# Hybrid decoder step (two layers, one core): every gathered key and value row is written to the new caches from SBUF, the copies leave these rows out

## The reference, cut to what matters

```python
kk = jnp.concatenate([k_buf, k], axis=1)
vv = jnp.concatenate([v_buf, v], axis=1)
o = dilated_attention(q, kk, vv, k_buf.shape[1])
new_k = kk[:, -n_keep:]
new_v = vv[:, -n_keep:]
```

## Time and profile before

| What | Value |
|---|---|
| Time, median of 3 runs | 415.51 us (415.07 to 419.36) |
| Time of the profiled execution | 418.61 us |
| Its span, first to last instruction | 416.8 us |
| PE matmul busy | 351.3 us (84%) |
| DVE, ACT, POOL busy | 232.5, 99.3, 46.2 us |
| DMA moved | 158.06 MB, mean 379 GB/s |
| HBM read, written | 149.39 MB, 104.42 MB |

### The profile page before, as it was taken

The page is one execution under the profiler, slowest core; times in us unless marked ns, Lnnn a source line. Parts: engine busy times, 40 slices in busy tenths (PEclk is TensorE's granted clock), DMA queues, the critical chain, the costliest instruction groups (busy, mean ns, idle before and its releaser), DMA issues.

```text
span 416.8 us, 4509 instructions
## 1 busy us (share of the span) xinstructions
PE 351.3 (84%) x1536; PEld 270.5 (65%) x1536; DVE 232.5 (56%) x522; ACT 99.3 (24%) x234; POOL 46.2 (11%) x87
## 2 busy tenths in 40 slices
PE   1489799977489979999979999997578969999980
PEld 1378688865367756558868888885356755558860
DVE  0334679749974776430123589849986786331010
ACT  3110014530152422410120021641233422310110
POOL 2300011111101111110100001112010111210000
PEclk9999999996878999999998999998969998999996
DMA  8999999999999999999999999999999999999972
GB/s 288 418 418 418 420 414 370 387 401 390 404 411 418 411 383 411 396 373 362 413 392 416 406 361 402 387 403 393 374 411 415 414 369 403 351 339 338 324 282 84
DMA packets 50676, 158.06 MB, mean 379 GB/s; under 512 B 4724, under 2 KB 20030, under 8 KB 49870
## 3 DMA queue, kind: packets, MB, share of 16 engines
q0 software_dynamic: 21824, 95.11, 59.3%
q1 hardware_dynamic: 19652, 39.36, 25.6%
q10 hardware_dynamic: 9178, 23.31, 14.3%
HBM read 149.39 MB, written 104.42 MB: 609 GB/s over the span
## 4 chain that ended last, share of the span: by engine, by line
SPq 38%; DMA 21%; PE 20%; DVE 16%; issue 2%; ACT 1%; ACTq 0%; DVEq 0%
SPq L380 15%; DMA kv<-in_cache_k_win 13%; DMA out<-kv 8%; PE pj L731 7%; SPq L405 6%; SPq L452 5%; SPq L435 5%; PE pj L592 4%; DVE kv L1096 4%; DVE ssc L1099 4%; PE psc L663 3%; DVE yc L1156 3%; SPq L391 3%; SPq L395 2%; PE ptr L508 2%
## 5 line engine op out<-in xcount | busy, mean ns | idle before, releaser
L592 PE MATMUL pj<-hT,w 128*128 128x264 f32 x800 | 195.6, 403 | 8.6 <-DVE hT L1018 6.0
L592 PEld LDWEIGHTS pj<-hT,w 128*128 128x128 f32 x800 | 157.8, 200 | 40.8 <-issue 10.1
L1156 DVE SCALAR_TENSOR_TENSOR yc<-u_ext,par,yc 128x256 f32<-128x256 f32 x180 | 76.2, 481 | 2.8 <-DVE u_smp L1046 0.6
L731 PE MATMUL pj<-mix,w 128*128 128x264 f32 x256 | 59.5, 387 | 0.0
L731 PEld LDWEIGHTS pj<-mix,w 128*128 128x128 f32 x256 | 48.0, 190 | 8.0
L496 POOL DMA_DIRECT2D out<-in_cache_v_win x48 | 25.8, 543 | 180.2 <-issue 180.2
L1226 DVE TENSOR_TENSOR xT<-xT,pj 128x264 f32<-128x264 f32 x16 | 6.9, 429 | 52.9 <-PE pj L731 52.9
L496 POOL DMA_DIRECT2D out<-in_cache_k_win x32 | 18.6, 584 | 138.4 <-issue 131.3
L840 ACT ACTIVATE ex<-pj 128x264 f32<-128x264 f32 x22 | 8.6, 391 | 82.1 <-PE pj L592 66.3
L663 PE MATMUL psc<-kv,spm 128*48 128x384 f32 x80 | 27.5, 496 | 0.0
L1096 DVE TENSOR_TENSOR kv<-kv,qb 128x1536 f32<-128x1536 f32 x10 | 17.6, 1759 | 10.3 <-DMA kv<-in_cache_k_win 10.0
(11 more groups left out here) (172 smaller groups left out, 322.9 us busy)
## 6 DMA issues: line engine op xcount, KB each, us to landing
out<-in_cache_k_win POOLq DMA_DIRECT2D x32, 1512.0 KB, 75.2
out<-in_cache_v_win POOLq DMA_DIRECT2D x16, 1152.0 KB, 75.4
out<-in_cache_v_win POOLq DMA_DIRECT2D x17, 1080.0 KB, 72.9
w<-in_w_out ACTq DMA_DIRECT2D x2, 4096.0 KB, 28.9
out<-in_cache_v_win POOLq DMA_DIRECT2D x16, 432.0 KB, 73.2
w<-in_w_in SPq DMA_DIRECT2D x2, 3072.0 KB, 32.4
w<-in_w_in ACTq DMA_DIRECT2D x1, 4608.0 KB, 30.7
kv<-in_cache_k_win SPq DMA_DIRECT2D x32, 144.0 KB, 25.1
```

Source lines behind the costliest of these rows:

```text
L592: last = nc.tensor.matmul(pj[n % RING][:, 0:T], wbuf[buf][:, k, col:col + P], hT[:, k, :], start=(k == 0), stop=(k == KD - 1))
L731: last = nc.tensor.matmul(pj[n % RING][:, 0:T], w1[:, k, m * P:(m + 1) * P], mix[:, k, :], start=(k == 0), stop=(k == KD - 1))
L1156: last = V.scalar_tensor_tensor(out=yc[:, t, 0:SEQ], in0=x_w, scalar=par[:, ROW_CW + w * CT + t:ROW_CW + w * CT + t + 1], in1=yc[:, t, 0:S ...
```

## The change

- `put_back` replaces `put_back_values`. Near, mid and far rows of keys and of values are written to the new caches from `kv`. For the far span, output row -1 does not exist, so its first row is left out: 15 partitions of each sample (90 rows) and then 2 DMAs for the 5 remaining rows of the first partition of the samples.
- The copies leave out all gathered rows: 15 of 16 rows up to 1535, 3 of 4 rows of 1536 to 1919, and none of the near ones, for keys and values alike, 48 DMAs a layer.
- On SP the keys' put-backs stand between the load of `w2` and the gather of the values. Each span's put-back waits for its keys (`k_near_in` and so on), and each span's gather of values waits now for the keys' put-back as well as for `ks_used`. The keys' gather of layer 1 waits for the values' put-back span by span.
- The key products no longer overwrite `kv`. They go to `tok4`, one tile that holds `v_tok` and `k_tok`, so DVE waits in layer 1 for these two tiles to have been written out, and ACT's first `vtok` copy waits for the last `sscore`. `sscore` 0, 2 and 3 each wait for one span of keys; before, `sscore` 0 waited for all.
- The last copies of y to SBUF wait for `v_near_out` alone.

```diff
+SPAN_AT = [sum(n for _, _, n in GATHER[:g]) for g in range(len(GATHER))]
+FIRST_CUT = [next(i for i, (a, b) in enumerate(SCORE_CUTS) if b > at) for at in SPAN_AT]
+LAST_CUT = [next(i for i, (a, b) in enumerate(SCORE_CUTS) if b >= at + g[2]) for at, g in zip(SPAN_AT, GATHER)]
...
-COPIES = [("k", s, a, a + HALF_ROWS) for s in range(NS) for a in (0, HALF_ROWS)]
-COPIES += [("v", s, a, b) for s in range(NS) for a, b in ((0, 768), (768, EVEN_ROWS), (FAR_LO, GATHER[0][0]))]
+COPIES = [(kind, s, a, b, d) for kind in "kv" for s in range(NS) for a, b, d in
+          ((0, GATHER[1][0] // 2, GATHER[2][1]), (GATHER[1][0] // 2, GATHER[1][0], GATHER[2][1]),
+           (GATHER[1][0], GATHER[0][0], GATHER[1][1]))]
+SPANS = ("near", "mid", "far")
...
-        v_tok = sb("v_tok", [P, 2, C_ATT])
-        k_tok = sb("k_tok", [P, 2, C_ATT])
+        tok4 = sb("tok4", [P, 4, C_ATT])
+        v_tok, k_tok = tok4[:, 0:2, :], tok4[:, 2:4, :]
...
+            def put_back(kind, l, g):
+
+                name = f"{kind}_{SPANS[g]}_out"
+                out = {"k": o_k_s, "v": o_v_s}[kind][bass.ds(l, 1)]
+                (lo, d, n), at = GATHER[g], SPAN_AT[g]
+                skip = 1 if lo == 0 else 0
+                for s in SAMPLE_ORDER:
+                    r = sample_rows(s)
+                    rows = out[:, s, lo - 1 + d * n * skip:lo - 1 + d * n * PER_S]
+                    rows = rows.rearrange("o (a b e) h d -> (o a) b e (h d)", b=n, e=d)[:, :, 0, :]
+                    sp.dma_start(rows, kv[r.start + 2 * skip:r.stop:2, at:at + n, :]).then_inc(S[name], 16)
+                if skip:
+                    for r in range(2):
+                        rows = out[:, r:NS:2, d - 1:d * n - 1]
+                        rows = rows.rearrange("o s (b e) h d -> (o s) b e (h d)", e=d)[:, :, 0, :]
+                        sp.dma_start(rows, kv[r:P:2 * PER_S, at + 1:at + n, :]).then_inc(S[name], 16)
...
                 sp.wait_ge(x_copied, XROUNDS)
                 if l > 0:
                     sp.wait_ge(S["sc_full"], nth(l - 1, "sc_full", NH + 1))
-                    for name in ("v_near_out", "v_far_out"):
-                        sp.wait_ge(S[name], nth(l - 1, name, per[name]))
-                gather("k", l, "k_in")
+                for g, span in enumerate(SPANS):
+                    if l > 0:
+                        sp.wait_ge(S[f"v_{span}_out"], nth(l - 1, f"v_{span}_out", per[f"v_{span}_out"]))
+                    gather("k", l, g, f"k_{span}_in")
                 if l > 0:
                     sp.wait_ge(S["pj_full"], nth(l - 1, "pj_full", NPROJ))
                 weights(l, w2, 0, "w_in", COL["b_val"], 2 * C_POOL, "b_in")
-                gather("v", l, "v_in", "ks_used")
+                for g, span in enumerate(SPANS):
+                    sp.wait_ge(S[f"k_{span}_in"], nth(l, f"k_{span}_in", per[f"k_{span}_in"]))
+                    put_back("k", l, g)
+                for g, span in enumerate(SPANS):
+                    sp.wait_ge(S["ks_used"], nth(l, "ks_used", LAST_CUT[g] + 1))
+                    sp.wait_ge(S[f"k_{span}_out"], nth(l, f"k_{span}_out", per[f"k_{span}_out"]))
+                    gather("v", l, g, "v_in")
...
                 sp.wait_ge(S["v_in"], nth(l, "v_in", per["v_in"]))
-                put_back_values(l)
+                for g in range(len(SPANS)):
+                    put_back("v", l, g)
...
-                    if a < FAR_LO or kind == "k":
-                        dst = out[l, s, a:b].rearrange("(c e r) h d -> c e (r h d)", c=16, r=PIECE_ROWS)
-                        src = cache[l, s, a + 1:b + 1].rearrange("(c e r) h d -> c e (r h d)", c=16, r=PIECE_ROWS)
...
+                    dst = out[l, s, a:b].rearrange("(c e f) h d -> c e (f h d)", c=16, f=d)[:, :, 0:(d - 1) * C_ATT]
+                    src = cache[l, s, a:b].rearrange("(c e f) h d -> c e (f h d)", c=16, f=d)[:, :, C_ATT:d * C_ATT]
                     pool.dma_start(dst, src, max_dma_last_dim=PIECE_ROWS * C_ATT * 4).then_inc(copy_out[n % IN_FLIGHT], 16)
-            cache, out = (t.rearrange("l s t h d -> (l s) (t h d)") for t in (ins["cache_k_win"], o_k_s))
-            pool.dma_start(out[:, 2 * HALF_ROWS * C_ATT:(PAST - 1) * C_ATT],
-                           cache[:, (2 * HALF_ROWS + 1) * C_ATT:]).then_inc(bulk_out, 16)
...
+                        if step == ("vtok", 0):
+                            act.wait_ge(S["ks_used"], nth(l, "ks_used", len(SCORE_CUTS)))
...
-            for name in ("v_near_out", "v_far_out"):
-                act.wait_ge(S[name], DEPTH * per[name])
+            act.wait_ge(S["v_near_out"], DEPTH * per["v_near_out"])
...
                         if i == 0:
-                            dve.wait_ge(S["k_in"], nth(l, "k_in", per["k_in"]))
+                            if l > 0:
+                                dve.wait_ge(S["v_out"], l * per["v_out"])
+                                dve.wait_ge(S["k_out"], l * per["k_out"])
                             dve.wait_ge(S["tr_free"], nth(l, "tr_free", TR["qb"] + 1))
-                        V.tensor_tensor(kv[:, a:b, :], kv[:, a:b, :], qb[:, None, :].to_broadcast([P, b - a, C_ATT]),
+                        for g, span in enumerate(SPANS):
+                            if FIRST_CUT[g] == i:
+                                dve.wait_ge(S[f"k_{span}_in"], nth(l, f"k_{span}_in", per[f"k_{span}_in"]))
+                        V.tensor_tensor(tok4[:, :, :], kv[:, a:b, :], qb[:, None, :].to_broadcast([P, b - a, C_ATT]),
                                         ALU.mult).then_inc(S["kprod_ok"], 1)
                         dve.wait_ge(S["kprod_ok"], nth(l, "kprod_ok", i + 1))
-                        last = V.tensor_reduce(ssc[:, a:b, :], kv[:, a:b, :].rearrange("p j (h d) -> p j h d", h=NH), AX.X, ALU.add)
+                        last = V.tensor_reduce(ssc[:, a:b, :], tok4[:, :, :].rearrange("p j (h d) -> p j h d", h=NH), AX.X, ALU.add)
```

More of the change, by code:

```diff
@@ L345, in trunk_program @@
         squared, diagonal_ok = sem("squared"), sem("diagonal_ok")
-        bulk_out, y_out = sem("bulk_out"), sem("y_out")
+        y_out = sem("y_out")
         copy_out = [sem(f"copy_out{i}") for i in range(IN_FLIGHT)]
@@ L368, in one @@
                 return ins[name][bass.ds(l, 1)]
[L370 to L392, removed]
+            def gather(kind, l, g, name):
+                (lo, d, n), at = GATHER[g], SPAN_AT[g]
+                for s in SAMPLE_ORDER:
+                    rows = one(f"cache_{kind}_win", l)[:, s, lo:lo + d * n * PER_S]
+                    rows = rows.rearrange("o (a b e) h d -> (o a) b e (h d)", a=PER_S, e=d)[:, :, 0, :]
+                    sp.dma_start(kv[sample_rows(s), at:at + n, :], rows).then_inc(S[name], 16)
@@ L472, in _ @@
             sp.dma_start(y_sample.rearrange("s t d -> (s t) d"), x_tok[0:NS, 2 * D_MODEL:3 * D_MODEL]).then_inc(y_out, 16)
-            sp.wait_ge(bulk_out, 16 * 3)
             for i in range(IN_FLIGHT):
                 sp.wait_ge(copy_out[i], 16 * DEPTH * len(COPIES) // IN_FLIGHT)
-            for name in ("v_near_out", "v_far_out", "v_out", "k_out", "new_out", "tail_out", "state_out"):
+            for name in ("k_near_out", "k_mid_out", "k_far_out", "v_near_out", "v_mid_out", "v_far_out", "v_out", "k_out", "new_out", "tail_out", "state_out"):
                 sp.wait_ge(S[name], DEPTH * per[name])
@@ L486, in _ @@
             for l in reversed(range(DEPTH)):
[L487 removed]
+                for i, (kind, s, a, b, d) in enumerate(COPIES):
                     n = (DEPTH - 1 - l) * len(COPIES) + i
                     cache, out = (ins["cache_k_win"], o_k_s) if kind == "k" else (ins["cache_v_win"], o_v_s)
[L490 to L503 removed]
+                    dst = out[l, s, a:b].rearrange("(c e f) h d -> c e (f h d)", c=16, f=d)[:, :, 0:(d - 1) * C_ATT]
+                    src = cache[l, s, a:b].rearrange("(c e f) h d -> c e (f h d)", c=16, f=d)[:, :, C_ATT:d * C_ATT]
+                    pool.dma_start(dst, src, max_dma_last_dim=PIECE_ROWS * C_ATT * 4).then_inc(copy_out[n % IN_FLIGHT], 16)
         @block.tensor
@@ L1229, in _ @@
                 assert chain[0] == DVE_LINKS, chain[0]
-            for name in ("v_near_out", "v_far_out"):
-                dve.wait_ge(S[name], DEPTH * per[name])
+            dve.wait_ge(S["v_near_out"], DEPTH * per["v_near_out"])
             dve.wait_ge(y_turned, 2)
```

16 lines of the change are left out of this document (3 added, 13 removed).

## The result

The changed kernel takes 460.01 us in the median (457.87 to 464.41, 4 runs), the kernel before, beside it, 417.28 (415.07 to 419.36, 4 runs). The ratio is 1.1038, with a 95% interval of 1.0926 to 1.1151: slower by 10%, as forecast. Some runs are disturbed, with a lower granted clock and a longer time; the ratios leave them out and the medians do not, so a ratio can differ by a point from the quotient of two medians. The profiled execution took 457.87 us, with a span of 456.1. The page's slices come first, as the earlier trace rows for before, then the queues, as the earlier trace rows.

What follows compares the result with a forecast made beforehand. Bytes and the engine chain ending in y were taken to end together. Span 416.8 + 48 + 2 - 4 = 462.8 us; 464.6 with 1.8 around it, 461.5 by the median, rounded to 460; range 434 to 474.

Steps and rivals of the forecast that it cites:

- Bytes and copies worth nothing: Copies lose 10.17 MB, put-backs add the same: +1.2 us engine time, bounds -4.6 to +1.2, not booked.
- Keys' put-back, layer 0: Put-backs ahead of the values in SP's queue delay PE's first use of them by 34 us, bounds +21 to +42.
- Waits that go: DVE's waits for keys, 10.0 us in all, go, but the gain ends before spv, which awaits values: worth 0.
- Values' put-back, layer 0: Far span adds about 15 us before layer 1's keys, about 8 given back; keys in at 325 us, no wait.
- Layer 1: Keys' put-back again delays the values: PE's first use at 395 us, +48 in all, 14 from layer 1.
- Tail: From PE's first layer 1 values to the end, 70.1 us before: slow matmuls +2, y's DMAs on empty queues -4.
- Slow matmuls: PE's first psc matmuls run slow after some 30 us of idleness: +1 to +3 us over both layers.
- A: Rival, half hidden: layer 0 costs 15 to 20 us, layer 1 nothing more; 433 us, chance 0.13.
- B: Rival, bytes alone decide: values still arrive by 157 and 347 us; 417 us, no change, chance 0.05.
- C: Rival, faster: values in time, less copying and DVE's saved waits reaching PE; 411 us, chance 0.05.
- D: Rival, worse: slower single-row writes beside copies plus uneven far DMAs in both layers; 480 us, chance 0.05.
- Uneven DMAs: By the skill's rule, far put-backs end 3 us later, three times on the path, some 469 us; left out of the sum.

Runs made afterwards that it cites:

- e1: Changed kernel with only the new product tile and per-span waits: no keys' put-back, values near and mid as before, copies as before; 415.69 us, ratio 1.0027.
- e2: e1 with the values' far rows also put back and left out of the copies; 424.96 us, ratio 1.0301.
- e3: Changed kernel with only the keys' near span put back, values near and mid, the other rows by copies; 432.82 us, ratio 1.0449.
- e7: Changed kernel with the load of w2 issued from ACT's queue behind c_gate instead of by SP; 456.72 us, ratio 1.0815.
- e12: e5 repeated in another group, beside e11 on one chip; 422.1 us, ratio 1.0039.
- e11: e2 repeated in another group, beside e12 on one chip; 427.72 us, ratio 1.022.
- e5: Changed kernel without the keys' put-backs and without copies of their rows, so gathered key rows are not written at all; 422.18 us, ratio 0.9994.
- e6: Changed kernel with each sample's far put-back cut as 16 partitions x 5 rows plus 15 single rows; 463.91 us, ratio 1.0991.
- e4: Changed kernel with the keys' put-backs issued from ACT's queue instead of SP's, same bytes; 449.43 us, ratio 1.0867.
- e9: Changed kernel with the copies asked to go in packets of 1 row instead of 3; 462.07 us, ratio 1.1016.

## Why the prediction was right

The time, 460.01 us, is the forecast's 460.0, and the mechanism that carries it was there: the keys' put-backs stand in SP's queue between `w2` and the values, and PE waits. The trace is in fact 6.7 us shorter than the sum (span 456.1 for 462.8). That the median fits better is luck: the profiled execution of before lay 3.1 us above its median, that of after 2.1 below. Luck too is that inside layer 1 two errors of the sum cancel.

- **Bytes and copies worth nothing.** As far as it can be seen, right: 158.07 MB moved, HBM reads 139.22 MB. The 10.17 MB that the copies lost went into q1. No run takes this term alone.
- **Keys' put-back, layer 0: +34 us.** Right, and somewhat too large: 29.1 at PE's first use. `w2` landed at 105.0 us, not 108.8. From there to the last value it took 81.0 us, for 45.5 + 37 in the sum. 154.3 was the place where the values had been; they came 31.7 us after that.
- **Waits that go: 0.** Right. DVE's wait for the keys is gone (0.6 us idle before its products, the line below, for 10.0 in the earlier trace rows). e1 shows that PE's earlier start buys nothing alone. The page's group of products after:

```profile
L1101 DVE TENSOR_TENSOR tok<-kv,qb 128x1536 f32<-128x1536 f32 x10 | 17.6, 1758 | 0.6 <-DVE qb L1059 0.2
```

- **Values' put-back, layer 0: 15 us, 8 given back, no wait.** Keys were in at 320.9 us (325 forecast) and `w2` at 338.6 (344), both without a wait of their own, so right in this kernel. e2 shows that this part was mis-sized by itself: alone it makes layer 1's values 18.7 us later, and the 8 us given back are not there. In the whole change keys moved from 280.8 to 320.9, of which 31.7 us came from layer 0, so only some 8 were left for this term; it is included in the +48.
- **Layer 1: +14 us.** Right: PE's first use came at 392.24 instead of 346.72, +45.5 for +48; 16.5 of these in layer 1. The values were in at 392.1, between the two estimates, 387 by the bytes and 399 by the queue. The estimate by the queue had the parts wrong. Its put-back was to end at 386, and the values to follow "almost alone" at 380 GB/s in 10 us. In the trace SP issues the last put-back by 361.2 and the gather from 361.33 on; that takes 30.8 us to its last landing, and while q0 was nearly done, in 380 to 390 us, q1 moved 2.17 MB, 217 GB/s. SP needs some 0.6 us to issue each of these DMAs of 144 KB, which by itself allows no more than some 240 GB/s (an estimate from these two numbers); whether the issuing is what limited q1 there was not tested. The 3 us that the sum gave to the turn from write to read had no row of before behind it; e3 has 5.7 us from issue to first landing.
- **Tail: +2 for slow matmuls, -4 for y.** Here the sizes were off, to the good side. From PE's first use to the end it took 63.9 us, for 70.1 before, and the -4 is -7.5: y's last DMA was issued at 453.26, and the program ended 2.8 us later, against 10.3 before (406.53 to 416.8). In all kernels in which q0 is done before y this stretch is 62.1 to 65.0 us; in e1, where copies last to the end, it is 72.9.
- **Slow matmuls.** The windows of after: stretch, its length, busy time of PE, PEld, DVE, ACT, POOL with their instructions, granted clock, share of DMA, GB/s.

```profile
150.00:186.00 36.00, 0.80 (x11) 0.56 (x9) 6.86 (x20) 2.15 (x2) 4.95 (x9) 0.55 1.01 379
186.00:190.00 4.00, 3.87 (x7) 1.29 (x8) 0.00 (x0) 0.00 (x0) 0.00 (x0) 0.50 1.01 411
...
392.00:396.00 4.00, 3.76 (x7) 1.30 (x8) 0.00 (x0) 0.00 (x0) 0.00 (x0) 0.52 0.75 197
```

PE was busy 0.80 us of 36, and the granted clock was 0.55; then its first matmuls of `psc` run at 0.50, half speed or 1.2 GHz, and 7 of them take 3.87 us. 16 `psc` matmuls took 7.75 us there against 5.36 for the next 16. In layer 1 they took 7.10, where the kernel before had taken 5.9 (346.72 to 352.6, its first ones slow as well). Against before this is +2.4 us in layer 0 and +1.2 in layer 1: 3.6 us over both for the 1 to 3 that were forecast.

**The rivals.** A (half hidden, 433 us) needed layer 0 to cost 15 to 20 us; it cost 29.1. B (bytes alone, 417 us) falls for layer 0, where DMA was full in either kernel and the values still came 31.7 us later; but in layer 1 bytes explain more than the queue does (387 for 392.1; e7; e12 against e11). C (faster) has half its test in e1: values in time, DVE's waits gone, and the time is the same, because the copies end at 411.8 us. e5 has less copying as well (0.9994), but its values are late in layer 1, so values in time with less copying were not tried. D (480 us, by single rows and uneven DMAs) falls with the time itself. No kernel here beats the one before.

**Uneven DMAs.** The prediction weighed a rule of the Trainium skill ("DMA: Bandwidth & Descriptors", section "Why a DMA increments its semaphore by 16 and not by 1"), that would have made the far put-backs 3 us later, three times. e6 removes the uneven shapes nearly (15 single rows remain a DMA of 15), and values land at 186.4 and 395.5 us instead of 186.0 and 392.1, in a group whose kernel before is some 2% slower. This case doesn't show the cost, and can't exclude one of 3 us at a place.

## What to carry to other kernels

Before a buffer that is to be refilled is written out first, count the bytes that get in front of the refill: those in the same queue where queues are the limit, those of all queues where the engines are full; and compare with the slack of the first consumer (here 2.8 and 1.3 us against delays of 29 and 16). A read saved from HBM brought nothing here, since the same bytes still go over the DMA engines, and a load moved to another queue helped only where the queue, not the sum of bytes, was the limit. Issue DMAs from an engine that has work only where its queue has room.

## What the runs showed that I had not expected

- A small DMA behind big ones holds the issuing engine: two of 6 KB took 13.65 and 14.64 us to issue on ACT (e4), one of 45 KB took 11.34 us (e7).
- Three adjoining rows of 1,536 bytes go as one packet even where the kernel asks for pieces of one row: 19,968 packets for 84.94 MB either way (e9). What did change is the time from issue to landing, 22.7 us for 61.7.
- From the landing of a write to the landing of the first read into the same slots it takes about 6 us if nothing else stands in the queue, and for 3.5 of them it moves no packet (e3).
- With the copies out of the way the gather did not fill the engines: q1 moved 217 GB/s in 380 to 390 us of the changed kernel, for the 380 that the sum had.
- One and the same kernel, that of before, differs by 2% between two chips (414.85 and 423.34 us).
